# Two transformer blocks in one kernel: four weight units interleaved behind a norm, one more unit prepared ahead, and two steps moved away from the norm

## What is computed

```python
mix = hybrid_mixer(x, w_in[l], attn_sinks[l], conv_w[l], w_branch_a[l],
                   w_branch_b[l], w_branch_c[l], w_out[l])
x = layer_norm(ALPHA * x + mix, ln1_g[l], ln1_b[l])
ffn = swiglu(x, w_ffn_gate[l], w_ffn_up[l], w_ffn_down[l])
x = layer_norm(ALPHA * x + ffn, ln2_g[l], ln2_b[l])
```

```python
h = h + HALF * gt1 * swiglu_2(ada_norm(h, g_ffn1[l], sh1, sc1), w1_ffn1[l], w3_ffn1[l], w2_ffn1[l])
u = ada_norm(h, g_mix[l], sh2, sc2)
...
h = h + gt2 * y
h = h + HALF * gt3 * swiglu_2(ada_norm(h, g_ffn2[l], sh3, sc3), w1_ffn2[l], w3_ffn2[l], w2_ffn2[l])
return rms_norm(h, g_final)
```

## Time and profile before

| | us |
|---|---|
| median of 3 runs | 3172.16 |
| lowest and highest run | 3169.38, 3178.53 |
| span of the profiled execution, first to last instruction | 3178.3 |
| profiled execution itself, the run of 3178.53 | 3178.5 |
| PE busy in the span | 2991.2 |
| DVE busy, ACT busy | 1963.0, 1243.8 |

### The profile page before, as it was taken

One profiled execution on the slowest core, in us unless ns is written; L12 is line 12 of the kernel. 1 busy time (PEld: TensorE's weight loads), 2 busy tenths in 40 slices (PEclk: granted clock), 3 DMA queues, 4 the chain that ended last, 5 costly groups with the idle time before them and its releaser, 6 DMA issues.

```text
span 3178.3 us, 47156 instructions
## 1 busy us (share of the span) xinstructions
PE 2991.2 (94%) x17434; PEld 2578.0 (81%) x17434; DVE 1963.0 (62%) x3156; ACT 1243.8 (39%) x2033; POOL 76.7 (2%) x149
## 2 busy tenths in 40 slices
PE   8988998988996999989889989999899998989898
PEld 8968998968996888877658877888788887869898
DVE  4557765557677756656753347575675645775655
ACT  4554444454445222233542233222332223654444
POOL 0000000000000000000000000000000000000000
PEclk9989999989998999999899999999999999999999
DMA  6515654515563444321103234344343432315454
GB/s 236 177 50 168 220 200 153 184 50 162 200 216 127 174 153 165 136 93 47 58 11 96 89 126 146 132 165 152 133 165 126 158 110 81 110 52 191 151 184 144
DMA packets 133235, 436.57 MB, mean 137 GB/s; under 512 B 14816, under 2 KB 23264, under 8 KB 132832
## 3 DMA queue, kind: packets, MB, share of 16 engines
q1 hardware_dynamic: 112208, 358.06, 33.3%
q0 software_dynamic: 20880, 76.56, 7.0%
HBM read 433.51 MB, written 1.05 MB: 137 GB/s over the span
## 4 chain that ended last, share of the span: by engine, by line
PE 87%; DVE 8%; ACT 2%; issue 1%; DMA 1%; SPq 0%; DVEq 0%; ACTq 0%; POOLq 0%
PE bank L1357 24%; PE bank L1359 23%; PE bank L1358 23%; PE bank L1317 3%; PE bank L1318 3%; PE bank L1319 3%; DVE wlo L786 1%; DVE acc L1130 1%; PE aux L1412 1%; PE bank L1524 1%; ACT whi L443 1%; PE aux L1508 1%; PE bank L1433 1%; PE aux L1346 1%; DMA gates<-in_w_ada 1%
## 5 line engine op out<-in xcount | busy, mean ns | idle before, releaser
L786 DVE TENSOR_TENSOR wlo<-raw,whi 128x1024 fp32r<-128x1024 f32 (+4 forms) x756 | 832.6, 1103 | 459.6 <-ACT whi L443 457.8
L443 ACT CAST whi<-raw 128x1024 fp32r<-128x1024 f32 (+4 forms) x756 | 708.0, 950 | 283.0 <-PE bank L1359 205.2
L1357 PE MATMUL bank<-uhi,whi 128*128 128x512 f32 (+1 forms) x2048 | 735.3, 359 | 2.6 <-DVE ylo L813 2.4
L1359 PE MATMUL bank<-uhi,wlo 128*128 128x512 f32 (+1 forms) x2048 | 734.2, 359 | 0.0
L1358 PE MATMUL bank<-ulo,whi 128*128 128x512 f32 (+1 forms) x2048 | 734.2, 358 | 0.0
L1357 PEld LDWEIGHTS bank<-uhi,whi 128*128 128x128 f32 x2048 | 386.7, 189 | 66.7 <-issue 3.3
L1358 PEld LDWEIGHTS bank<-ulo,whi 128*128 128x128 f32 x2048 | 386.7, 189 | 63.3 <-issue 0.2
L1359 PEld LDWEIGHTS bank<-uhi,wlo 128*128 128x128 f32 x2048 | 386.6, 189 | 63.0
L1357 PE MATMUL bank<-x1hi,whi 128*128 128x256 f32 x1520 | 429.9, 283 | 3.0 <-DVE wlo L786 2.9
L1358 PE MATMUL bank<-x1lo,whi 128*128 128x256 f32 x1520 | 427.2, 281 | 0.0
L1359 PE MATMUL bank<-x1hi,wlo 128*128 128x256 f32 x1520 | 427.1, 281 | 0.0
(11 more groups left out here) (273 smaller groups left out, 4019.2 us busy)
## 6 DMA issues: line engine op xcount, KB each, us to landing
raw<-in_w_stream SPq DMA_DIRECT2D x580, 512.0 KB, 3.4
big<-in_w_ada POOLq DMA_DIRECT2D x66, 512.0 KB, 3.6
vt<-in_w_ada POOLq DMA_DIRECT2D x56, 512.0 KB, 3.6
raw<-in_w_stream SPq DMA_DIRECT2D x80, 256.0 KB, 2.7
raw<-in_w_stream SPq DMA_DIRECT2D x48, 384.0 KB, 3.0
gates<-in_w_ada POOLq DMA_DIRECT2D x22, 512.0 KB, 4.4
raw<-in_w_stream SPq DMA_DIRECT2D x32, 192.0 KB, 2.3
raw<-in_w_stream SPq DMA_DIRECT2D x16, 128.0 KB, 2.0
```

Source lines behind the costliest of these rows:

```text
L443: sc.copy(whi[:, u % SLOTS, 0:n], raw[:, u % SLOTS, 0:n]).then_inc(s_high, 1)
L786: ve.tensor_tensor(wlo[:, u % SLOTS, 0:n], raw[:, u % SLOTS, 0:n], whi[:, u % SLOTS, 0:n].bitcast(F32), ALU.subtract).then_inc(s_low, 1)
L1357: te.matmul(out_, whi[:, u % SLOTS, w], hi(k)[:, c0:c1], start=k == 0, stop=False)
L1359: ins = te.matmul(out_, wlo[:, u % SLOTS, w], hi(k)[:, c0:c1], start=False, stop=k == plan.kt[u] - 1)
```

## The change

AHEAD becomes 4, so each of ACT and DVE prepares unit j+4 beside unit j. In the written-out stages ACT now casts after it has evacuated, since unit j+4 takes the slot of unit j. `two_units` is replaced by `first_units` with two orders. `four_units`, which takes the place of late=8, interleaves units 0 to 3 for k = 0 to 4 (EARLY = 5), then finishes them one after the other (k = 5 to 7 of unit 0, of unit 1, and so on). `two_units` stays for the down stages and does the same products as before in nearly the same order. The preload of the root's table is moved ahead of the stage that precedes the norm. In the second stack the last weight residual is moved behind `add_square(7)` on DVE; in the first stack the new argument `late` and the separate call give the same place as before, directly behind the last evacuation and sum.

```diff
--- before.py
+++ after.py
@@ -30,7 +30,8 @@
 EPS = 1e-6
 
 SLOTS = 4
-AHEAD = 3
+AHEAD = 4
+EARLY = 5
 SLOT = 8 * P
 
 
@@ -514,7 +515,6 @@
                 stream(u0, plan.count[f"{stage}{c}"], 4, evac)
 
             def norm1(g, b, last):
-                sc.preload_act_table(ACT.Sqrt)
                 for m in range(0, DT, 2):
                     val.wait(1)
                     sc.activation(lg[:, m:m + 2, :], x1[:, m:m + 2, :], ACT.Square).then_inc(s_nsq, 1)
...
@@ -561,9 +561,9 @@
                     act.wait_ge(s_c, 16)
                     sc.activation(cs[:, :, :], cs[:, :, :], ACT.Silu).then_inc(s_aval, 1)
                 for j in range(24):
-                    high(u2 + j + AHEAD)
                     done(u2, j, 0, 0)
                     sc.activation(gates[:, j, :], bank(u2, j)[:, 0:S], ACT.Sigmoid).then_inc(read(u2, j), 1)
+                    high(u2 + j + AHEAD)
                     if j == CONV_AT + 10:
                         val.wait(1)
                         sc.copy(y1hi[:, 4:8, :], bbb[:, 8:12, :]).then_inc(s_ahi, 1)
@@ -579,10 +579,13 @@
                         val.wait(1)
                         sc.copy(x1hi[:, 4 * i + j // 3, :], lg[:, 3 + (j // 3) % 2, :]).then_inc(s_ahi, 1)
                 stream(U[f"merge{l}"], 24, 12, evac_m, [(val, 4)])
+                sc.preload_act_table(ACT.Sqrt)
                 stream(U[f"out{l}"], 8, 4, lambda j, i: None)
                 norm1(p1("ln1_g", l, DT), p1("ln1_b", l, DT), False)
                 for c, n in enumerate(CHUNKS):
                     hidden(f"up{l}", c, 0, S, lambda k: lg[:, k, :], lambda k: lg[:, 2 + k, :], y1hi)
+                    if c == len(CHUNKS) - 1:
+                        sc.preload_act_table(ACT.Sqrt)
                     stream(U[f"down{l}{c}"], 8, 4, lambda j, i: None)
                 norm1(p1("ln2_g", l, DT), p1("ln2_b", l, DT), l == L - 1)
 
@@ -600,10 +603,12 @@
                 def evac(j, i):
                     if 4 * i + j:
                         square(4 * i + j - 1, c0, u0)
+                sc.preload_act_table(ACT.Sqrt)
                 stream(u0, 8, 4, evac)
 
             def norm2(l, which, c0, ready):
-                sc.preload_act_table(ACT.Sqrt)
+                if not ready:
+                    sc.preload_act_table(ACT.Sqrt)
                 for m in range(DT - 1 if ready else 0, DT):
                     square(m, c0, ready)
                 stat.wait(1)
...
@@ -786,7 +791,7 @@
                 ve.tensor_tensor(wlo[:, u % SLOTS, 0:n], raw[:, u % SLOTS, 0:n],
                                  whi[:, u % SLOTS, 0:n].bitcast(F32), ALU.subtract).then_inc(s_low, 1)
 
-            def stream(u0, n, per, evac, tallies=()):
+            def stream(u0, n, per, evac, tallies=(), late=0):
                 iters = n // per
 
                 def body(i):
@@ -797,7 +802,8 @@
                 repeat(dve, iters - 1, body, tallies)
                 for j in range(per):
                     evac(j, iters - 1)
-                    low(u0 + n - per + j + AHEAD)
+                    if j < per - late:
+                        low(u0 + n - per + j + AHEAD)
 
             def done(u0, j, i, per):
                 dve.wait_ge(s_used, u0 + j + per * i + 1)
@@ -986,7 +992,9 @@
                             step.add(ins)
                         else:
                             ins.then_inc(s_dop, 1)
-                stream(u0, 8, 4, evac)
+                stream(u0, 8, 4, evac, (), int(last))
+                if last:
+                    low(u0 + 7 + AHEAD)
 
             for l in range(L):
                 for u in range(U[f"qkv{l}"], U[f"qkv{l}"] + 18):
@@ -1038,9 +1046,11 @@
             dve.wait_ge(s_mid, DT)
 
 
-            def norm2(l, which, c0):
+            def norm2(l, which, c0, after=None):
                 for m in range(0 if l == which == 0 else DT - 1, DT):
                     add_square(m, c0)
+                if after:
+                    low(U[after] + 7 + AHEAD)
                 if which is not None:
                     w = 3 * which
                     dve.wait_ge(s_ada_mod, plan.ada_iterations(DT * (NADA * l + w + 2)))
@@ -1097,7 +1107,7 @@
                     ins.then_inc(read(u0, j), 1)
                     if c1 is not None and m:
                         add_square(m - 1, c1)
-                stream(u0, 8, 4, evac)
+                stream(u0, 8, 4, evac, (), int(c1 is not None))
 
             def ffn2(l, f, c0):
                 for c, n in enumerate(CHUNKS):
@@ -1192,9 +1202,9 @@
             for l in range(L):
                 last = l == L - 1
                 c0 = S if last else 0
-                norm2(l, 0, 0)
+                norm2(l, 0, 0, f"fdown2{l - 1}2" if l else None)
                 ffn2(l, "1", 0)
-                norm2(l, 1, 0)
+                norm2(l, 1, 0, f"fdown1{l}2")
                 u0 = U[f"mix{l}"]
                 conv = Convolution(l, c0)
                 dve.wait_ge(s_used, u0 + 1)
...
@@ -1302,35 +1312,40 @@
             te = nc.tensor
             split, sq, dop, aop, prob, pt = (Tally(pe, s) for s in (s_split, s_sq, s_dop, s_aop, s_prob, s_pt))
 
-            def two_units(u, hi, lo, c0, c1, late=8):
-
-
-                n = plan.kt[u]
-
-                def start(v):
-                    pe.wait_ge(s_low, v + 1)
-                    if plan.freed(v):
-                        pe.wait_ge(s_free[v % SLOTS], plan.freed(v))
+            def first_units(u, spans, order, hi, lo):
+
+
+                seen = 0
 
                 def products(v, k):
+                    c0, c1 = spans[v - u]
+                    if k == 0:
+                        pe.wait_ge(s_low, v + 1)
+                        if plan.freed(v):
+                            pe.wait_ge(s_free[v % SLOTS], plan.freed(v))
                     w, s, out_ = slice(k * P, (k + 1) * P), v % SLOTS, banks[v % SLOTS][:, c0:c1]
                     te.matmul(out_, whi[:, s, w], hi(k)[:, c0:c1], start=k == 0, stop=False)
                     te.matmul(out_, whi[:, s, w], lo(k)[:, c0:c1], start=False, stop=False)
-                    ins = te.matmul(out_, wlo[:, s, w], hi(k)[:, c0:c1], start=False, stop=k == n - 1)
-                    if k == n - 1:
+                    ins = te.matmul(out_, wlo[:, s, w], hi(k)[:, c0:c1], start=False, stop=k == plan.kt[v] - 1)
+                    if k == plan.kt[v] - 1:
                         ins.then_inc(s_used, 1)
 
-                start(u)
-                for k in range(n - late):
-                    split.wait(1)
-                    products(u, k)
-                start(u + 1)
-                for k in range(n - late):
-                    products(u + 1, k)
-                for k in range(max(n - late, 0), n):
-                    split.wait(1)
-                    products(u, k)
-                    products(u + 1, k)
+                for j, k in order:
+                    if k == seen:
+                        split.wait(1)
+                        seen += 1
+                    products(u + j, k)
+
+            def four_units(u, spans, hi, lo):
+
+                early = [(j, k) for k in range(EARLY) for j in range(4)]
+                first_units(u, spans, early + [(j, k) for j in range(4) for k in range(EARLY, plan.kt[u])], hi, lo)
+
+            def two_units(u, hi, lo, c0, c1):
+
+                n = plan.kt[u]
+                order = [(j, k) for j in range(2) for k in range(n - 1)] + [(j, n - 1) for j in range(2)]
+                first_units(u, [(c0, c1)] * 2, order, hi, lo)
 
             def by_token(src, t0, t1):
 
@@ -1385,8 +1400,12 @@
                 iters = n // per
                 first = 0
                 if ready:
-                    two_units(u0, lambda k: hi(0, k), lambda k: lo(0, k), c0, c1, late)
-                    for j in range(2, per):
+                    begun = 4 if late == 8 else 2
+                    if begun == 4:
+                        four_units(u0, [(c0, c1)] * 4, lambda k: hi(0, k), lambda k: lo(0, k))
+                    else:
+                        two_units(u0, lambda k: hi(0, k), lambda k: lo(0, k), c0, c1)
+                    for j in range(begun, per):
                         unit(u0, j, 0, 0, lambda k: hi(j, k), lambda k: lo(j, k), c0, c1)
                     first = 1
 
@@ -1450,8 +1469,8 @@
             for l in range(L):
                 u0 = U[f"qkv{l}"]
                 hi_, lo_ = (lambda k: x1hi[:, k, :]), (lambda k: x1lo[:, k, :])
-                two_units(u0, hi_, lo_, 0, S)
-                for j in range(2, 18):
+                four_units(u0, [(0, S)] * 4, hi_, lo_)
+                for j in range(4, 18):
                     if j == 5:
                         units_v(u0 + j, 1, hi_, lo_, QT)
                     elif j >= 14:
@@ -1558,8 +1577,8 @@
                 ffn2(l, "1", 0)
                 norm2(0)
                 u0 = U[f"mix{l}"]
-                two_units(u0, lambda k: uhi[:, k, :], lambda k: ulo[:, k, :], 0, T2)
-                for j in range(2, 16):
```

(2 more changed lines are left out.)

10 lines of the change are left out of this document (5 added, 5 removed).

## The result

The changed kernel takes 3183.4 us (median of 20 runs, 3177.0 to 3188.6); the kernel before, timed beside it, 3176.7 us (20 runs, 3168.7 to 3181.1). The ratio is 1.0022, 95% interval 1.0014 to 1.0030: slower by 7 us (4.4 to 9.5). My 3171.5 us with a range up to 3183 is missed. 4.5 us of that is the median of before itself, 3176.7 here and 3172.2 in the three runs I had; the rest is a loss where I forecast a gain of 0.7 us.

A forecast was written before the change was run, and what follows sets the result against it. The prediction took PE's stream to bound the kernel, busy 2991.2 of 3178.3 us. Its terms summed to a gain of 0.7 us, from the median of 3172.2 to 3171.5 us, range 3158 to 3183.

The forecast's parts named there:

- The start: Program start: PE waits for weights of units 2 and 3; -3.0 us, ends -4.8 and -1.6.
- The residual behind the last sum of squares: Second-stack norms: last sum starts earlier, 0.87 us at four norms and 0.5 at another; +4.0 us.
- The chain of the norm is not shorter: Rival, second-stack norms: the cast before the square replaces the residual, so +4.0 becomes 0; 3175.5 us, chance 0.12.
- The first stack's norms: First-stack norms: the residual waits for its cast and delays centring, 0.3 us four times; -1.2 us.
- The table: Root's table load, second-stack norms: PE's last unit hides it, so moving it gains 0.
- The gate's tail: Gate stage end: residual delays softmax biases and the second attention's scores, -1.6 us in each of two layers; -3.2 us.
- the merge: Merge stage, bound by DVE: one more ready unit lets PE end about 1.3 us earlier, two layers; +2.6 us.
- Mix, kv and q: These three stages: DVE's later work and PE's saved waits taken as 0 together; ends -3 and +3 us.
- The slower rival: Mix: DVE's own work comes a unit late and kv starts late; 3182.6 us, chance 0.16.
- The faster rival: Starts behind norms and residual waits: full clock returns sooner, one more unit covers waits; 3161.5 us, chance 0.22.
- Four units instead of two ... 0: Interleaved starts: same products in another order, no wait inside the old order to fill; 0 us.
- up10: Stage up10: one more unit covers DVE's condition-weight wait, though unit 0 finishes later; +1.5 us, ends -2.5 and +3.9.

The follow-up runs named there:

- e2: Kernel before, with only the second-stack norms' residual moved behind the last sum of squares and the root's table loaded earlier: ratio 0.9978, 3168.5 us.
- e4: First stack exactly as in the kernel before, second stack as in the changed kernel: ratio 0.9987.
- e12: e6 with four units interleaved at nine of twelve starts (not the program's first, up00 or up10): ratio 0.9985.
- e10: The same kernel as e6, timed again on another chip: ratio 0.9988.
- e5: Changed kernel, but stages up00 and up10 of the first stack begin with two units interleaved: ratio 1.0005, 3176.4 us.
- e1: Changed kernel, but the first stage of the program begins with two units interleaved: ratio 1.0013, 3178.0 us.
- e16: Changed kernel with first-stack condition-weight transfers cut to 16 of 128 partitions (wrong modulation values in the second stack), timed again: ratio 1.0004.
- e17: e5 with condition-weight transfers cut to 16 of 128 partitions, timed again beside e16: ratio 0.9985.
- e3: Changed kernel with four units kept ready, but two instead of four interleaved at every start: ratio 0.9989, 3172.6 us.
- e7: e6 with the last unit's residual in the first-stack norms put between the centring and the sums of squares: ratio 0.9985.
- e6: e3 with the gate stage's last residual put behind the softmax biases of both attentions: ratio 0.9970, 3163.9 us.
- e9: e6 with the last unit's residual in the first-stack norms put behind the last low part of the activations: ratio 0.9974.

## Why the prediction was wrong

- **The start**, -3.0, was right in sign, and the trace gives 3.7 us, inside its ends. The two waits are 2.25 and 0.13 us. (The lower end, -4.8, is 0.3 us more than its two parts, 3.0 and 1.5.)
- **The residual behind the last sum of squares**, +4.0, was right: 0.78 us at four norms and 0.34 at the fifth (I had 0.87 and 0.5), and 0.1 us before the first matmuls, 4.0 in all. "The chain of the norm is not shorter" is refuted by the wait of 2.52 us and by e2.
- **The first stack's norms**, -1.2, were right with 1.1 us.
- **The table**, 0: no wait of ACT for it is on a chain in after. It was not tested by itself; e2 holds this move too.
- **The gate's tail**, -3.2, **and the merge**, +2.6: the mechanism of the first is right, 1.30 us a layer. The merge gains 0.6 us a layer, not 1.3, because PE then stands for 1.32 us at the stage's end. Together they are -1.4 us where I had -0.6.
- **Mix, kv and q**, 0, are right as a sum, as far as e4 shows it. The first taps start at 1488.9 us, 2.7 us later beside PE. The slower rival that named mix as its place is refuted by e4. The total came out on its side, 3183.4 against its 3182.6, for another reason, and that is luck.
- **The faster rival**, the clock by denser starts, is refuted: the half clock in the eleven starts is as long in after as in before (47.7 and 49.5 us), and e12, which has four units at nine more starts than e10, is as fast. By the Trainium skill's page "TensorE: Matmul & The Clock Gate", section "Why this matters for your kernels", the loop nest should be dense; these starts were already dense, which is what the earlier trace rows said.
- **The step that failed is "Four units instead of two ... 0", and with it up10, +1.5.** At the stages up00 and up10 four units are a loss: 5.4 us with full transfers (the changed kernel against e5, not side by side), 6.2 us on one chip (e5 against e1, with the start's 3.7 us counted), and 6.0 us with short transfers (e16 against e17). With all eleven later starts it is 7.6 us (e1 against e3, one chip), and nine of them by themselves cost nothing (e12). I had seen that unit 0 is done later and had priced it as the low end of up10 alone, -2.5 us, hidden under a gain; I left it out at up00. It was also counted wrong: in the order before unit 0 is done after 45 matmuls and not 48, and units 1 to 3 after 48, 72 and 96, so the new order makes unit 0 late by 24 matmuls and unit 1 by 30. The further unit that was to cover DVE's wait in up10 brought nothing by the ratios.

With measured terms my sum is -3.7 + 4.0 - 1.1 - 1.4 - 5.4 + 0 = -7.6 us, and the measurement is -7.0. The place and the size of the failed term are shown by the runs. Its way is shown only in part: beside the clock, most of the cost goes when the transfers are short, but long waits for transfers come with two units too (e10, e12), and of the 6 us between e16 and e17 some 4 are half clock that nothing here ties to the order. The measured 3183.4 us also holds 4.5 us that belong to no step, because the median of the three runs of before that I had is 4.5 us below that of the twenty.

## What to carry to other kernels

Interleaving more pieces of work delays the first result: before interleaving more units where a norm ends, ask what waits for the first of them. PE was never idle inside these starts, so it had nothing to gain. A piece of work that is moved out of a chain belongs where its engine waits for another engine's answer, behind the last instruction that the chain needs; between two links that overlap (e7) it costs more than it did before. Price each part alone: the norm's part of this change gives 4 to 7 us by itself (e2), and two units with four ready and two or three residuals moved give 4 to 10 (e6, e9, e10), while all of it together loses 7.
